# mLSTM output gates in two groups of four PSUM banks, with the first head pair's preparation between the units of the second group

## What is computed

```python
qk, v, og, g = jnp.split(h @ w_in, [o1, o2, o3], axis=-1)
qk = jax.nn.silu(_centred_conv(qk, conv_w, conv_b))
...
hn = _head_norm(h_sum.transpose(0, 2, 1, 3)).reshape(b, s, -1) * norm_g
return (jax.nn.sigmoid(og.astype(jnp.float32)) * hn).astype(og.dtype) @ w_out
```

## Time and profile before

| what | us |
|---|---|
| median of 3 runs | 1905.59 (1902.66 to 1906.91) |
| the profiled execution, its own time | 1901.86 |
| its span, first to last instruction | 1900.1 |
| TensorE busy in it | 1776.1 |
| VectorE, ScalarE, GpSimd busy | 688.1, 607.5, 716.1 |

### The profile page before, as it was taken

The page is one execution under the profiler, slowest core; times in us unless marked ns, Lnnn a source line. Parts: engine busy times, 40 slices in busy tenths (PEclk is TensorE's granted clock), DMA queues, the critical chain, the costliest instruction groups (busy, mean ns, idle before and its releaser), DMA issues.

```text
span 1900.1 us, 24466 instructions
## 1 busy us (share of the span) xinstructions
PE 1776.1 (93%) x9848; PEld 1424.3 (75%) x9848; DVE 688.1 (36%) x1187; ACT 607.5 (32%) x863; POOL 716.1 (38%) x378
## 2 busy tenths in 40 slices
PE   4999999899899999999999996999776989999998
PEld 2788767455588888888888883787565878888886
DVE  2134254566467511111111036750178761111114
ACT  1531322455435411022111125451324453122124
POOL 0442200266456423233332242343225764445435
PEclk8999999999999999999999997999878999999999
DMA  8412132355312222121221126222100323333322
GB/s 295 121 47 62 58 122 89 103 165 177 111 56 65 58 67 78 56 67 57 76 58 53 50 61 207 56 69 66 55 1 23 89 70 108 111 89 100 88 83 72
DMA packets 210986, 163.36 MB, mean 86 GB/s; under 512 B 17742, under 2 KB 191022, under 8 KB 210902
## 3 DMA queue, kind: packets, MB, share of 16 engines
q1 hardware_dynamic: 208320, 157.77, 27.8%
q10 hardware_dynamic: 2582, 4.42, 0.6%
HBM read 160.08 MB, written 2.10 MB: 85 GB/s over the span
## 4 chain that ended last, share of the span: by engine, by line
PE 82%; DVE 10%; ACT 4%; issue 2%; DMA 2%; POOL 1%; ACTq 0%; POOLq 0%; DVEq 0%
PE ps L692 58%; PE ps L680 3%; PE ps L682 3%; PE ps L681 3%; PE ps L851 2%; PE ps L878 2%; PE ps L903 1%; PE ps L888 1%; PE ps L805 1%; DMA ring<-in_mod_w 1%; PE ps L634 1%; PE ps L644 1%; DVE xT L2002 1%; PE ps L789 1%; DVE xT L1992 1%
## 5 line engine op out<-in xcount | busy, mean ns | idle before, releaser
L2375 POOL TENSOR_TENSOR wsplit<-ring,wsplit 128x1024 fp32r<-128x1024 f32 (+1 forms) x136 | 326.0, 2411 | 521.2 <-ACT wsplit L1470 521.0
L692 PE MATMUL ps<-hhi,wsplit 128*128 128x512 f32 (+1 forms) x1920 | 473.1, 354 | 6.4 <-DVE hu L2041 6.4
L692 PEld LDWEIGHTS ps<-hhi,wsplit 128*128 128x128 f32 x1920 | 314.9, 188 | 60.0 <-DVE hu L2041 6.9
L692 PE MATMUL ps<-hlo,wsplit 128*128 128x512 f32 x960 | 288.0, 354 | 0.0
L692 PE MATMUL ps<-uhi,wsplit 128*128 128x512 f32 x1008 | 250.4, 353 | 0.0
L2118 DVE TENSOR_TENSOR hu<-sg,ps 128x768 f32<-128x768 f32 (+1 forms) x40 | 32.9, 821 | 438.1 <-ACT sg L1539 438.1
L1470 ACT ACTIVATE wsplit<-ring 128x1024 fp32r<-128x1024 f32 (+1 forms) x136 | 135.1, 1023 | 173.5 <-PE ps L692 173.5
L692 PEld LDWEIGHTS ps<-uhi,wsplit 128*128 128x128 f32 x1008 | 164.9, 188 | 27.6
L692 PEld LDWEIGHTS ps<-hlo,wsplit 128*128 128x128 f32 x960 | 157.5, 188 | 26.5
L1965 DVE SCALAR_TENSOR_TENSOR xT<-ps,modc,xT 128x512 f32<-128x512 f32 x96 | 60.6, 659 | 272.1 <-PE ps L692 250.4
L692 PE MATMUL ps<-ulo,wsplit 128*128 128x512 f32 x504 | 150.8, 353 | 0.0
(11 more groups left out here) (355 smaller groups left out, 2713.9 us busy)
## 6 DMA issues: line engine op xcount, KB each, us to landing
ring<-in_mod_w SPq DMA_DIRECT2D x96, 512.0 KB, 4.8
ring<-in_ffn_w_in SPq DMA_DIRECT2D x88, 512.0 KB, 3.9
ring<-in_ffn_w_out SPq DMA_DIRECT2D x32, 512.0 KB, 4.1
ring<-in_m_w_in SPq DMA_DIRECT2D x24, 512.0 KB, 3.7
ring<-in_ab_w_in SPq DMA_DIRECT2D x21, 512.0 KB, 4.0
ring<-in_ffn_w_out SPq DMA_DIRECT2D x16, 384.0 KB, 3.5
ring<-in_ab_w_out SPq DMA_DIRECT2D x8, 512.0 KB, 4.6
ring<-in_m_w_out SPq DMA_DIRECT2D x8, 512.0 KB, 3.7
```

The lines of the kernel that those rows point to most:

```text
L692: mm = pe.matmul(dst[:, a:b], w, h[:, a:b], start=st, stop=sp_)
L2375: pool.tensor_tensor(w_part(s, 1)[:, 0:width], ring[:, (NB[f"ffn{l}"] + s) % RING, 0:width], w_part(s, 0)[:, 0:width].bitcast(F32), ALU.su ...
```

## The change

The gate columns are done in two groups of 512 (heads 0 to 3, then 4 to 7), each of four units with two k chunks of 512 columns, so that a group fills four banks: group 0 banks 0 to 3, group 1 banks 4 to 7. While group 1 accumulates, banks 0 to 3 are free: after its first unit (20) TensorE runs `key_rows(0)` and `max_rows(0, 0)`, after unit 21 `query_rows(0)` and `max_rows(0, 1)`, after unit 22 `m_scores(0)`, after unit 23 nothing more. ScalarE does the first group's four sigmoids (128x512 each) after split 21, the exponentials of pair 0 around split 23, and the second group's sigmoids last; GpSimd does the first two selects ahead of the low part of unit 23. The value units 12 to 15 use other banks, and the evacuations count differently. In SBUF, `mo`, `qs`, `pe` and `states` are each divided in two, so that what group 1's units still read (`hlo1`, `wlo1`) isn't overwritten by pair 0's tiles. The core of the diff (left out: where only a name changes, `qs[:, p % 2, ...]` to `qs[p % 2][:, ...]` and the like, and the argument `between` in the head of `token_major`):

```diff
@@ -246,8 +246,11 @@
 ...
     hlo1_raw = under(("hlo1_raw", [P, KD, T], F32))
-    mo = sb("mo", [P, LT, H_M * M_DV], at=m1)
-    qs = sb("qs", [P, 2, 2, LAT], at=m1)
+
+    mo_b = sb("mo_b", [P, LT, H_M // 2 * M_DV], at=m1)
+    pe_b = sb("pe_b", [P, 2, 2, LAT], at=m1)
+    qs_b = sb("qs_b", [P, 2, LAT], at=m1)
+    hbt = sb("hbt", [P, 2, 2, 2, M_DV], at=m1)
...
@@ -263,21 +266,27 @@
     gt = sb("gt", [P, 2, T], at=ph)
     gbc = sb("gbc", [P, 2, T], at=ph)
     wr = lf
+    sb("qx_pad", [P, 8], at=ph)
     qx = sb("qx", [P, 2, LAT], F32R, at=ph)
     ph.close()
     ph = phase()
 
     _, wsp_out1 = under(("wsp_out1_pad", [P, 816], F32), ("wsp_out1", [P, 2, 2, UNIT], F32R))
-    pe_ = sb("pe", [P, 2, 2, 2, LAT], at=ph)
-    kw = sb("kw", [P, 2, 2, TT, P], at=ph)
-    stt_ = sb("states", [P, 2, 2, LT, M_DV + 1], at=ph)
-    hbt = sb("hbt", [P, 2, 2, 2, M_DV], at=ph)
-    dab = sb("dab", [P, 2, 2, 2], at=ph)
-    dcol = sb("dcol", [P, 2, 2, LT], at=ph)
     mst = sb("mst", [P, LT * H_M, 6], at=ph)
     mmv = sb("mmv", [P, LT * H_M, 2], at=ph)
     mrs = sb("mrs", [P, LT * H_M], at=ph)
-    oT_b = sb("oT_b", [P, 2, LAT], F32R, at=ph)
+    dab = sb("dab", [P, 2, 2, 2], at=ph)
+    st_b = sb("states_b", [P, 2, LT, M_DV + 1], at=ph)
+    sb("wlo_rest", [P, 2 * UNIT + 1 - (LT * H_M * 9 + 8 + 2 * LT * (M_DV + 1))], at=ph)
+    pe_a = sb("pe_a", [P, 2, 2, LAT], at=ph)
+    qs_a = sb("qs_a", [P, 2, LAT], at=ph)
+    kw = sb("kw", [P, 2, 2, TT, P], at=ph)
+    st_a = sb("states_a", [P, 2, LT, M_DV + 1], at=ph)
+    oT_b = under(("oT_b", [P, 2, LAT], F32R))
+    mo_a = sb("mo_a", [P, LT, H_M // 2 * M_DV], at=ph)
+    dcol = sb("dcol", [P, 2, 2, LT], at=ph)
+
+    pe_, qs, stt_, mo = (pe_a, pe_b), (qs_a, qs_b), (st_a, st_b), (mo_a, mo_b)
     ph.close()
     m1.close()
 
@@ -590,11 +599,10 @@
             slot_free(n)
             if i < 8:
                 unit(n, view(n % RING, KD), w_in[:, :, i * P:(i + 1) * P])
-            elif i >= 16:
-                unit(n, ring[:, n % RING, :], w_in[:, i - 16, C_MO:C_MO + H_M * M_DV])
             else:
                 g, q = (i - 8) // 4, (i - 8) % 4
-                unit(n, view(n % RING, 2), w_in[:, 2 * q:2 * q + 2, C_MV + g * 512:C_MV + (g + 1) * 512])
+                c0 = (C_MV, C_MV + 512, C_MO, C_MO + 512)[g]
+                unit(n, view(n % RING, 2), w_in[:, 2 * q:2 * q + 2, c0:c0 + 512])
...
@@ -762,6 +770,9 @@
                         cols = slice(t * P, (t + 1) * P)
                         mm = three(half(b), ((h_hi[:, k, cols], w_hi), (h_lo[:, k, cols], w_lo)), k == 0, k == KD - 1)
                 mm.then_inc(unit_done, 1)
+                if between:
+                    for part in between[q]:
+                        part(0)
 
         in0_parts = ((wsp_in0[:, 0], wsp_in0[:, 1]), hx[:, 0], hx[:, 1])
         token_major("in0", NF, [(0, 0), (1, 1), (4, 4), (5, 5), (2, 2), (3, 3)], *in0_parts,
@@ -1103,26 +1114,18 @@
                 at = (4 * LT + d * TT + t) * H_M
                 mm = pe.transpose(half(7)[:, at:at + H_M], wr[0:H_M, d, t * P:(t + 1) * P], ident[0:H_M, 0:H_M])
         mm.then_inc(tr_mm, 1)
-        v1 = {6: lambda: None, 7: lambda: pe.wait_ge(tr_ev, 3), 0: lambda: pe.wait_ge(vg_ev, 1), 1: lambda: pe.wait_ge(vg_ev, 1),
-              2: lambda: pe.wait_ge(vg_ev, 2), 3: lambda: pe.wait_ge(vg_ev, 2)}
-        token_major("in1", 12, [(0, 6), (1, 7), (2, 0), (3, 1), (4, 2), (5, 3)], *in1_parts, lambda b: v1[b]())
-
-        for k in range(KD):
-            split_unit("in1", 16 + k)
-            for b in (4, 5, 6, 7, 0, 1, 2, 3):
-                if k == 0:
-                    pe.wait_ge(vg_ev, {2: 3, 3: 4, 0: 5, 1: 6}[b // 2])
-                cols, c0 = slice((b // 2) * P, (b // 2 + 1) * P), 512 * (b % 2)
-                mm = three(half(b), ((hT1[:, k, cols], whi1[:, k % 2, c0:c0 + 512]), (hlo1[:, k, cols], wlo1[:, k % 2, c0:c0 + 512])),
-                           k == 0, k == KD - 1)
-            mm.then_inc(unit_done, 1)
+        v1 = {6: lambda: None, 7: lambda: pe.wait_ge(tr_ev, 3), 4: lambda: pe.wait_ge(vg_ev, 1), 5: lambda: pe.wait_ge(vg_ev, 1),
+              0: lambda: pe.wait_ge(vg_ev, 2), 1: lambda: pe.wait_ge(vg_ev, 2)}
+        token_major("in1", 12, [(2, 6), (3, 7), (0, 4), (1, 5), (4, 0), (5, 1)], *in1_parts, lambda b: v1[b]())
+
+        token_major("in1", 16, [(2, 2), (3, 3), (0, 0), (1, 1)], *in1_parts, lambda b: pe.wait_ge(vg_ev, 4 - b // 2))
 
 
         def key_rows(p):
             if p:
                 pe.wait_ge(m_st, p)
             else:
-                pe.wait_ge(vg_ev, 10)
+                pe.wait_ge(vg_ev, 8)
                 pe.wait_ge(silu_ev, 8)
...
@@ -1134,7 +1137,7 @@
             elif p:
                 pe.wait_ge(m_st, p)
             else:
-                pe.wait_ge(vg_ev, 9)
+                pe.wait_ge(vg_ev, 7)
                 pe.wait_ge(sel_ok, 1)
                 pe.wait_ge(nx_lo, 1)
             for d in range(2):
@@ -1174,7 +1177,7 @@
         def m_values(i):
             p, c = divmod(i, LT)
             if i < 2:
-                pe.wait_ge(vg_ev, 8)
+                pe.wait_ge(vg_ev, 9 + i)
             else:
                 pe.wait_ge(m_num, i - 1)
             if c == 0:
@@ -1189,19 +1192,17 @@
...
-        key_rows(0)
-        max_rows(0, 0)
-        query_rows(0)
-        max_rows(0, 1)
-        m_scores(0)
+
+        token_major("in1", 20, [(2, 6), (3, 7), (0, 4), (1, 5)], *in1_parts, lambda b: pe.wait_ge(vg_ev, 5 if b >= 6 else 6),
+                    ((key_rows, lambda p: max_rows(p, 0)), (query_rows, lambda p: max_rows(p, 1)), (m_scores,), ()))
         m_updates(0)
         for p in range(1, NP + 1):
             i = LT * (p - 1)
@@ -1649,20 +1650,28 @@
...
-        pairs = ((0, 1, 2), (3, 0, 1))
+
+        pairs = (((2, 2), (0, 0), (1, 1)), ((2, 0), (1, 3), (0, 2)))
         for g in range(2):
             for i in range(11 if g == 0 else 14, 14 + 4 * g):
                 split_high("in1", i, whi1)
-            for i, b in enumerate(pairs[g]):
+            for i, b in pairs[g]:
                 for q in range(2):
                     ins = act.activation(mv[:, 2 * i + q, 4 * g:4 * g + 4, 0:M_DV],
                                          half(2 * b + q).rearrange("p (h d) -> p h d", h=4), ACT.Copy)
                 ins.then_inc(vg_ev, 1)
-        for i in range(18, N_IN1):
+
+        def out_gates(g):
+            act.wait_ge(unit_done, UB["in1"] + 20 + 4 * g)
+            for t in range(LT):
+                ins = act.activation(mo[g][:, t, :], half(4 * g + t), ACT.Sigmoid)
+                if t % 2:
+                    ins.then_inc(vg_ev, 1)
+
+        for i in range(18, 22):
             split_high("in1", i, whi1)
-        act.wait_ge(unit_done, UB["in1"] + N_IN1)
-        for t in (2, 3, 0, 1):
-            act.activation(mo[:, t, :], PS[t][:, :], ACT.Sigmoid).then_inc(vg_ev, 1)
+        out_gates(0)
+        split_high("in1", 22, whi1)
         act.wait_ge(tr_ev, 3)
 
         def m_inverse_std(i):
@@ -1679,11 +1688,13 @@
...
         m_exps(0, 0)
+        split_high("in1", 23, whi1)
         m_exps(0, 1)
+        out_gates(1)
         for p in range(1, NP + 1):
             i = LT * (p - 1)
             if p < NP:
@@ -2434,6 +2446,14 @@
...
+        def m_select(p, b):
+            for d in range(2):
+                pool.wait_ge(mexp, 4 * p + 2 * b + d + 1)
...
+                pool.affine_select(out=blk, in_=blk, pattern=[[0, LT], [sign, P]], compare_op=ALU.is_ge, fill=0.0, base=0,
+                                   channel_multiplier=-sign).then_inc(msel, 1)
+
         pool.wait_ge(z_ev, ZB[1])
         pool.memset(wg[:, :, :, :].bitcast(F32), 0.0).then_inc(gate_zero, 1)
         split_low("in1", 0, whi1, wlo1)
@@ -2452,15 +2472,10 @@
                 pool.wait_ge(gate_mm, 1)
                 pool.wait_ge(sel_ok, 1)
                 pool.memset(mv[:, :, :, M_DV:M_DV + 1], 1.0).then_inc(ones_ok, 1)
+            if i == N_IN1 - 2:
+                m_select(0, 0)
             if 4 <= i < 4 + KD:
                 residual_chunk(1, i - 4)
-        def m_select(p, b):
...
         def m_normalise(p):
             pool.wait_ge(mrstd, p + 1)
```

More of the change, by code:

```diff
@@ L750, in _, with token_major @@
                 rotate(f - 6, half(6 + (f - 6) % 2), rot_ret, rot_source(f - 1), 0, P, rope_mm, rope_ev)
-        def token_major(stage, i0, banks, wsp, h_hi, h_lo, ready):
+        def token_major(stage, i0, banks, wsp, h_hi, h_lo, ready, between=()):
             for q in range(4):
@@ L933, in m_source @@
         def m_source(c, t):
-            return mo[:, t, c * P:(c + 1) * P]
+            return mo[c // 4][:, t, c % 4 * P:(c % 4 + 1) * P]
         def out_projection(l, source, h_lo, wsp):
@@ L1191, in m_values @@
                     rows = slice(M_DK * b, M_DK * (b + 1))
-                    pe.matmul(dst(b, d), qs[rows, p % 2, d, cols], stt_[rows, p % 2, d, n, :], start=(d == 0), stop=False,
```

(45 more changed lines are left out.)

## The result

The changed kernel takes 1890.9 us (median of 14 runs, 1883.6 to 1899.6) against 1906.0 (14 runs, 1897.9 to 1912.8) for the kernel before. The ratio is 0.9922, with a 95% interval of 0.9903 to 0.9942: 15 us faster, between 11 and 18.5. Forecast were 18.8 us less and 1886.8. The measured time lies in the range of 1882 to 1893, but outside the 1884 to 1889 that had a chance of 0.73.

The account below looks back on a forecast made before the run. TensorE was taken as the bound (busy 93% of the span), waiting on hand-offs after the output gates. Savings of 16.4 + 2.4 = 18.8 us gave 1883.1 profiled; the median's 3.7 more gave 1886.8, range 1882 to 1893.

Parts of the forecast that it names:

- first term: From the old end of the output gates to the first state copy: 6.55 us instead of 22.97, 16.4 us saved.
- The covers: Units 20 to 23: other engines finish before TensorE needs each insert's inputs, cost 0; thinnest margin 1.2 us, for the sigmoids.
- Second term: Next head pair (pair 1): VectorE's two waits for output matmuls shrink by 1.2 us each, 2.4 saved; bounds 0 and 3.9.
- rival 1: The clock falls anyway in pair 1, so only the first 16.4 us are saved: 1889.2 us; chance 0.12.
- Rival 3: Units 21 to 23: the inserts bring TensorE's clock down, 5.6 us slower than before, 1911; chance 0.03.
- rival 2: A cover is too thin: a hand-off stalls units 21, 22 or 23 by 1 to 5 us, 1888 to 1892; chance 0.08.
- larger gain: Whole kernel: a gain larger than the forecast sum of 18.8 us; chance 0.02.

Follow-up runs that it names:

- Sigmoids late: Changed kernel with ScalarE's split of unit 22 ahead of the first group's sigmoids; 60.5 us from split of unit 17 to first state copy, against 52.2.
- scores last: Changed kernel with pair 0's scores behind unit 23 instead of between units 22 and 23; 56.4 us from split of unit 17 to first state copy.
- the updates inside: Changed kernel with pair 0's 40 updates mid unit 23; ratio to kernel before 0.9919. A second version adds unused matmuls in later TensorE waits: 1888.9 us, 0.9900.
- ten extra matmuls: Changed kernel plus ten unused 512-column matmuls behind pair 0's updates, filling TensorE's pause; ratio to kernel before 0.9895, pair 1 in 15.9 us.

## Why the prediction was right, and where it was not

- *Mechanism and first term.* Right. From the start of an insert to the next gate matmul it took 1.4 us for key transposes and rows (forecast 1.6), 1.1 for the query rows and rows (1.4) and 1.1 for the scores (1.05); the updates took 2.4 (2.42). From the start of split 17 to the first copy 16.57 us were saved for 16.4.
- *The covers.* Right, all of them: no wait of TensorE between units 20 and 23. The thinnest, of the sigmoids, was forecast at 1.2 us and is 0.9. "Sigmoids late" and "scores last" show that the covers are what earns the gain: without one, 8.3 and 4.3 us are lost.
- *Second term.* Wrong. The step was "2.4 us saved if the clock is still up when this pair runs", taken as likely because the pause of some 2.5 us is no longer than TensorE's idle time in 1404 to 1412, where the clock was 1.00. It fell in both profiles of the changed kernel, so this was rival 1, which had a chance of 0.12: by its sum 1889.2, nearer to the measured 1890.9 than the forecast. Two readings of the kernel before had failed. The 2.41 us of idle in 1404 to 1412 are one wait of 0.82 and the first 1.6 of a longer one, which runs on past the window's end and behind which the scores took 2.08 us instead of 1.1:

```profile
1414.44 2.08 PE L1157 MATMUL ps<-mq,mk 64*128 64x128 f32 x16 [4.03 <-ACT pe L1682]
```

  And the low clock of pair 1 did not outlive the gap of 1358.9 to 1377.2: it was back at 1.00 near the end of the updates (1381.3), stayed there through the state chain's pause, and fell again just behind it (1.00 in 1382 to 1384, 0.50 in 1386 to 1394, above). The pause that the forecast took to be harmless brought the clock down in that very trace. The size was off as well: with the clock up, the pair takes 15.9 us, so the term is 3.6 and near its upper bound of 3.9. The two waits of VectorE for the output matmuls, priced at 1.2 us each, nearly vanish (3.9 to 0.4 us).
- *Rival 3 and the rule named there.* The inserts as such did not bring the clock down: the stage ran at 1.00, with three inserts of other kinds of matmul. What does is a wait at an insert, shown by "sigmoids late". The Trainium skill (TensorE: Matmul & The Clock Gate, section on a second failure mode by psum-queue cycling) speaks of short idles between groups; here, groups with only their issue gaps between them left the clock alone. The forecast named the wait ahead of 1372.45 as one of some 4 us; it is 2.27, and the waits of about 4 us are the ones ahead of 1362.67 (3.86) and 1414.44 (4.03).
- *The rest.* The gate's regrouping cost nothing, as forecast, and neither did the loads in pieces of two chunks or the two extra table loads. Later pairs and the output projection moved earlier as a block: 156.1 to 139.6 us, 16.5.
- *Total.* 15 us measured, with an interval that holds 16.5 and only just not 18.8. That the range holds the time is in part luck: its upper end, 1893, was set by stalls at the covers (rival 2), which no profile of the changed kernel shows. Two small slips in the chances: forecast and rivals 1 and 2 add up to 0.93, with the larger gain to 0.95, not 0.94; and the 2.5 units at which rival 3 decides would be 2.9 by the units alone, and about 2 with the inserts and updates at half clock too.

## What to carry to other kernels

Work that hops between engines is worth placing between the units of a long matmul stage, one hop after each unit, when every engine's part fits in a unit: it costs the matmuls' own time and hides the rest. Count the clock with it, in both directions: a filled wait gives back the low clock behind it (4.7 us here with no overlap at all), and an insert that has to wait costs more than its wait (8.3 us for 4.6). If the next pause can't be hidden, a few matmuls that nobody reads, into a free bank, may be worth as much as a further move: by the profiles 3.7 us here, against 3.8 for the updates inside the unit. And before a short pause is called harmless, look in the trace at the clock behind each pause of that length, and let the window run to the end of the pause.

## What the runs showed of the hardware that was not expected

The same matmuls of one stage ran at two paces in different executions, both at a granted clock of 1.00. Over 300 us of the first feed-forward stage, where TensorE never waits, the kernel before has

```profile
760.00:1060.00 300.00, 300.00 (x1733) 262.35 (x1732) 35.47 (x48) 52.90 (x58) 83.73 (x35) 1.00 0.21 61
```

and the version with the updates inside, whose code is the same there,

```profile
760.00:1060.00 300.00, 300.00 (x1700) 260.20 (x1699) 35.90 (x48) 52.91 (x57) 83.37 (x35) 1.00 0.21 60
```

That is 1733 against 1700 matmuls, 1.9%. Four of the twelve profiles have the slower pace (ten extra matmuls, sigmoids late, and both with the updates inside), eight the faster, among them both of the changed kernel. From the first to the last group of this stage's matmuls it is 525.5 us in the four, and 517.2 in the others (515.6 in the kernel before): 8.3 us. The second layer's feed-forward stage takes 338.9 to 340.0 us in all twelve, so the slower pace did not last for the whole execution. It makes spans differ without any difference in the stage that was changed, and can be a part of the spread of the timed runs (1883.6 to 1899.6). It does not explain the 4.5 us by which the stage began later in the changed kernel's profile, since both profiles have the faster pace. What sets it, and whether it goes with a kernel or with an execution, wasn't settled. And the same pause of 2.5 us of TensorE left the clock up in one execution and brought it down in five.
